# A two-layer transformer step on one core: eight chunks of the adaptive weights come first, sixteen move into the first merge

## The chip, the core and the metric

The kernel runs on one core of a Trainium2 chip. Its time is the device time of one execution, in microseconds (us). TensorE multiplies; ScalarE (ACT), VectorE (DVE) and GpSimd (POOL) work on tiles in SBUF; SyncE (SP) issues the transfers. Each engine runs its own instructions in order and waits for the others on semaphores. [...]

## The reference

The program computes two blocks of two layers each. The change touches the first block only. There, each layer takes a shift, a scale and a gate from a condition vector, for the 256 tokens `x` and the 256 context tokens `ctx`:

```python
for l in range(DEPTH):
    mod = jax.nn.silu(c) @ w_ada[l] + b_ada[l]
    mod_c = jax.nn.silu(c_ctx) @ w_ada[l] + b_ada[l]
    shift, scale, gate = jnp.split(mod[:, None, :], 3, axis=-1)
    ...
    h = rms_norm(x, norm_g[l]) * (1.0 + scale) + shift
    ...
    x_new = x + gate * y
```

`w_ada[l]` is 1024 x 3072. `c` and `c_ctx` are inputs, so the shifts, scales and gates of both layers depend on nothing that the kernel computes before. The gate is wanted only where the layer's output is added to `x`.

## The kernel before

All weights come from one array, `wstream`, in chunks of 1 MB, in the order in which they are used. Four ring buffers hold chunks (`ring`). Each chunk is split for accuracy: ACT rounds it into an upper part `w_hi` (L207, two halves), DVE subtracts to get the rest `w_lo` (L219, two halves), both into the one of two buffers that the chunk's parity picks. TensorE then multiplies three times per weight tile (upper by upper, upper by lower, lower by upper; L261 to L263). SP loads chunk c + 4 once chunk c is split.

A layer of the first block runs in stages, each a block of instructions for every engine that ends when all engines have arrived:

- `ada_stage`: 12 chunks of `w_ada`. The condition vectors (`c_both`, both as upper and lower parts, padded to 128 columns) are the stationary operand and 256 columns of weights stream past (L314, L315); the result is a row of numbers on 4 partitions, copied to `rows` (L476). From the ninth chunk on ACT also squares the eight tiles of `x` (L482), and TensorE sums the squares (L430). In layer 0 the stage also loads `x`, the context, the small parameters and the constants.
- `mod_stage`: TensorE turns the rows into columns (L369, 24 small transposes), ACT takes the inverse root of the mean square (L497, L499), DVE makes `mod` and `scales`, and then multiplies the eight tiles of `x` by the root (L401). In layer 0 a table of biases is also built and stored to device memory (L363), and the stage ends only when the store has landed.
- `glu_stage`: tile by tile, ACT applies scale and shift (L518), POOL rounds the result to `x_hi` (L525), DVE takes the rest `x_lo` (L530), and TensorE starts on tile k of the first chunk when `x_lo` of k is there (`model_norm`).
- the projections and the attention, and then `merge_stage`: 28 chunks (gate, merge and projection for three branches, and four output chunks), each 48 matmuls. Results alternate between the two sides of PSUM. In layer 0 it covers 512 tokens.

For layer 1 the same stages run again, its `ada_stage` directly behind layer 0's `merge_stage`.

## Time and profile before

| | us |
|---|---|
| three runs | 2562.76, 2568.67, 2569.83 |
| median | 2568.67 |
| the profiled execution | 2568.35 |
| its span in the trace | 2566.6 |
| `ada_stage` of layer 0 | 10.0 to 62.6 |
| `mod_stage` of layer 0 | 62.6 to 70.7 |
| `merge_stage` of layer 0 | 352.5 to 676.7 |
| `ada_stage` of layer 1 | 677.3 to 716.4 |
| `mod_stage` of layer 1 | 716.4 to 724.6 |

Stage borders are read from the first instruction of a stage in the trace, in us from the start of the span. A stage's time is what separates its borders; what an engine does inside it costs something only if it is what the stage's end waits for.

### The profile page before, as it was taken

The numbers are of one execution on the slowest core, as the hardware profiler recorded it, in microseconds if no ns is written. First come the engines' busy times: TensorE is split into PE (matmuls) and PEld (weight loads), VectorE is DVE, ScalarE is ACT, GpSimd is POOL, SyncE is SP. The second block draws the span as 40 slices with busy tenths as digits, with TensorE's granted clock in tenths as the row PEclk, the third lists the DMA queues.
The fourth block names the chain that finished last, engine by engine and source line by source line (L and its number), as shares of the span: only waits on it lengthen the run. The fifth ranks groups of instructions, "written<-read, shape, count | busy, mean of one in ns | idle before, by whom it ended". The sixth has DMA issues, their size and how long they took to land. (4 is left out here: it accounts for less than half of the span.)

```text
span 2566.6 us, 45931 instructions
## 1 busy us (share of the span) xinstructions
PE 2408.7 (94%) x17574; PEld 2171.2 (85%) x17574; DVE 1482.7 (58%) x2652; ACT 1247.7 (49%) x1964; POOL 214.3 (8%) x228
## 2 busy tenths in 40 slices
PE   5899899999989999999989999999999988998998
PEld 4678567887767789989987789899899887898998
DVE  4468963333566865655465556554555566565554
ACT  6355654232457565434365454543543564555433
POOL 0013000000002100023000000121121000000220
PEclk9999899999989999999999999999999999999999
DMA  8221022222452125555543234355455442343552
GB/s 334 80 96 70 1 83 93 96 103 88 166 177 96 37 99 181 181 183 193 182 159 116 95 136 164 141 188 183 145 184 193 144 165 83 121 160 132 188 189 98
DMA packets 58453, 354.04 MB, mean 138 GB/s; under 512 B 5904, under 2 KB 16704, under 8 KB 16832
## 3 DMA queue, kind: packets, MB, share of 16 engines
q1 hardware_dynamic: 58160, 351.96, 38.4%
q8 instruction: 104, 1.70, 0.3%
q14 instruction: 45, 0.37, 0.0%
q10 hardware_dynamic: 144, 0.01, 0.0%
HBM read 349.29 MB, written 1.08 MB: 137 GB/s over the span
## 5 line engine op out<-in xcount | busy, mean ns | idle before, releaser
L219 DVE TENSOR_TENSOR w_lo<-ring,w_hi 128x1024 fp32r<-128x1024 f32 x644 | 823.5, 1313 | 517.6 <-ACT w_hi L207 517.4
L261 PE MATMUL psum<-x_hi,w_hi 128*128 128x256 f32 (+1 forms) x3392 | 1043.2, 308 | 60.2 <-DVE x_lo L615 21.9
L263 PE MATMUL psum<-x_hi,w_lo 128*128 128x256 f32 (+1 forms) x3392 | 1024.5, 302 | 0.0
L262 PE MATMUL psum<-x_lo,w_hi 128*128 128x256 f32 (+1 forms) x3392 | 1023.4, 302 | 0.0
L207 ACT ACTIVATE w_hi<-ring 128x1024 fp32r<-128x1024 f32 (+1 forms) x644 | 650.0, 1051 | 299.8 <-PE psum L1573 143.9
L261 PEld LDWEIGHTS psum<-x_hi,w_hi 128*128 128x128 f32 x3392 | 647.4, 191 | 105.5 <-issue 64.7
L262 PEld LDWEIGHTS psum<-x_lo,w_hi 128*128 128x128 f32 x3392 | 648.8, 191 | 27.6 <-issue 2.2
L263 PEld LDWEIGHTS psum<-x_hi,w_lo 128*128 128x128 f32 x3392 | 648.3, 191 | 23.9
L1573 PE MATMUL psum<-h_hi,w_lo 128*128 (+1 forms) x640 | 179.0, 280 | 0.0
L1572 PE MATMUL psum<-h_lo,w_hi 128*128 (+1 forms) x640 | 178.7, 279 | 0.0
L1570 PE MATMUL psum<-h_hi,w_hi 128*128 (+1 forms) x640 | 178.6, 279 | 0.0
L1594 ACT ACTIVATE gate<-psum 128x256 f32<-128x256 f32 x88 | 33.8, 385 | 279.3 <-PE psum L263 279.2
L796 ACT ACTIVATE probT<-psum 128x512 f32<-128x512 f32 (+3 forms) x128 | 79.8, 623 | 179.9 <-PE psum L713 179.2
L1640 POOL CAST h_hi<-hid 128x256 f32 (+1 forms) x88 | 35.0, 397 | 1320.2 <-DVE hid L1613 1320.2
L811 ACT ACTIVATE prob<-prob,neg 128x256 f32<-128x256 f32 (+6 forms) x256 | 127.9, 503 | 34.9 <-DVE neg L764 28.3
L1231 DVE SCALAR_TENSOR_TENSOR conv_out<-cpad,vec,conv_out 128x512 f32<-128x512 f32 (+1 forms) x240 | 142.9, 652 | 0.0
L1613 DVE SCALAR_TENSOR_TENSOR hid<-psum,gate 128x256 f32<-128x256 f32 x88 | 37.4, 425 | 145.6 <-ACT gate L1594 145.5
L1572 PEld LDWEIGHTS psum<-h_lo,w_hi 128*128 128x128 f32 x640 | 120.3, 188 | 0.0
L1573 PEld LDWEIGHTS psum<-h_hi,w_lo 128*128 128x128 f32 x640 | 120.0, 188 | 0.0
L1570 PEld LDWEIGHTS psum<-h_hi,w_hi 128*128 128x128 f32 x640 | 119.8, 187 | 0.0
L1642 POOL TENSOR_TENSOR h_lo<-hid,h_hi 128x256 f32 (+1 forms) x88 | 109.7, 1247 | 13.5 <-POOL h_hi L1640 12.7
L713 PEld LDWEIGHTS psum<-cst,prob 128*128 128x128 f32 (+1 forms) x544 | 60.9, 141 | 44.2 <-DVE prob L771 40.8
(292 smaller groups left out, 2968.6 us busy)
## 6 DMA issues: line engine op xcount, KB each, us to landing
ring<-wstream SPq DMA_DIRECT2D x323, 1024.0 KB, 4.8
x<-xT SPq DMA_DIRECT2D x2, 1024.0 KB, 7.1
x<-ctxT SPq DMA_DIRECT2D x2, 1024.0 KB, 9.9
rel_bias<-bias_by_distance SPq DMA_DIRECT2D x2, 1024.0 KB, 7.6
cst<-consts SPq DMA_DIRECT2D x1, 1662.0 KB, 11.6
kk_sw<-kk_sw SPq DMA_DIRECT2D x8, 128.0 KB, 5.9
out<-x SPq DMA_DIRECT2D x8, 128.0 KB, 2.0
x<-rpb SPq DMA_DIRECT2D x2, 438.0 KB, 5.9
```

The source lines that it names most:

```text
L207: act.activation(w_hi[:, c % 2, h], ring[:, (c + 2 * i) % RING, h], ACT.Copy).then_inc(hi_done.sem, 1)
L219: dve.tensor_tensor(w_lo[:, c % 2, h], ring[:, (c + 2 * i) % RING, h], w_hi[:, c % 2, h].bitcast(F32), ALU.subtract).then_inc(split_done.s ...
L261: pe.matmul(o, w_hi[:, c, w_cols], hi, start=first, stop=False)
L262: pe.matmul(o, w_hi[:, c, w_cols], lo, start=False, stop=False)
L263: return pe.matmul(o, w_lo[:, c, w_cols], hi, start=False, stop=last)
L796: act.activation(self.probT[0:w, v % self.TURNS, :, 0:n], psum[0:w, at:at + wide].rearrange("p (h k) -> p h k", h=2)[:, :, 0:n], ACT.Copy) ...
L811: o = act.activation(p, p, ACT.Exp, bias=self.neg[:, t % 3, half:half + 1], accum_out=self.den[:, t % 3, half:half + 1])
L1231: dve.scalar_tensor_tensor(out=o, in0=src, scalar=wc, in1=o, op0=ALU.mult, op1=ALU.add).then_inc(conv_step.sem, 1)
L1570: pe.matmul(o, w_hi[:, c, b:b + P], h_hi[:, kt, :], start=start and k == 0, stop=False)
L1572: pe.matmul(o, w_hi[:, c, b:b + P], h_lo[:, kt, :], start=False, stop=False)
L1573: mm = pe.matmul(o, w_lo[:, c, b:b + P], h_hi[:, kt, :], start=False, stop=False)
L1642: pool.tensor_tensor(h_lo[:, j, :], hid[:, s, :], h_hi[:, j, :].bitcast(F32), ALU.subtract).then_inc(lower.sem, 1)
```

## The change

Layer 0's `ada_stage` runs 8 chunks (shift and scale) instead of 12. The other 16 (layer 0's gate, 4 chunks, and all 12 of layer 1) are placed in layer 0's `merge_stage`, one behind each main chunk from the third to the eighteenth. Their results go to a free corner of PSUM and then to the first four partitions of `x`, which is not in use there; `x` is loaded again later in the stage. The rows are turned behind main chunks 6 (8 transposes) and 18 (24). Layer 1 has no `ada_stage` and no `mod_stage`: ACT squares `x` during the output chunks, DVE adds the first six of the eight squares into one (five adds), TensorE sums that one and the last two in three matmuls, and the root is taken at the end of `merge_stage`. `c_both` has 4 columns instead of 128 and stays. The multiplication by the root moves, for both layers, from `mod_stage` into `model_norm`, in `glu_stage`, between the `x_lo` steps. The constants come in two parts, and `x` is loaded earlier. In the woven stretch the main chunks all lie in one of the two weight buffers, the ada chunks in the other, so a main chunk's halves are split apart: the first once TensorE has read the first half of the main chunk before (`half_read`), the second once it is done.

```diff
+ADA_FIRST = 8
+ADA_LATER = 2 * ADA_CHUNKS - ADA_FIRST
...
+                    if half_read and n == CB // 2 - 1:
+                        mm.then_inc(half_read.sem, 1)
...
+        def condition(dve, c_both):
+            c0 = conditioned.n
+            upper_half, lower_half = c_both[:, :, 0:2], c_both[:, :, 2:4]
+            dve.tensor_copy(upper_half, c_in[:]).then_inc(conditioned.sem, 1)
+            dve.wait_ge(conditioned.sem, c0 + 1)
+            dve.tensor_tensor(lower_half, c_in[:], upper_half.bitcast(F32), ALU.subtract).then_inc(conditioned.sem, 1)
...
+        def turn_rows(pe, rows, n, at):
+            for t in range(n):
+                mm = pe.transpose(psum[:, at + 4 * t:at + 4 * t + 4], rows[:, t * P:t * P + P], const("ident")[0:4, 0:4])
+            mm.then_inc(rows_turned.sem, 1)
...
-                    dve.wait_ge(rooted.sem, r0 + 2)
-                    for k in range(KT):
-                        dve.tensor_tensor(scratch(k), x[:, k, :], rs[:], ALU.mult).then_inc(scaled_x.sem, 1)
...
+            squares = {5: range(2), 6: range(2, 5), 7: range(5, 8)}
...
+                            sp.dma_start(cst[:, 0:early], consts[:, 0:early]).then_inc(loaded.sem, 16)
                             sp.dma_start(vec[:], vecs).then_inc(loaded.sem, 16)
-                        if j == 6:
-                            sp.dma_start(cst[:], consts[:, 0:N_RESIDENT]).then_inc(loaded.sem, 16)
-                        if j == 7:
-                            rel_sb, bucket, _tab = tables
                             sp.dma_start(rel_sb[:], rel).then_inc(loaded.sem, 16)
                             sp.dma_start(bucket[:], consts[0:32, N_RESIDENT:N_CONST]).then_inc(loaded.sem, 16)
+                        if j == 4:
+                            sp.dma_start(cst[:, early:], consts[:, early:N_RESIDENT]).then_inc(late_consts.sem, 16)
...
+                        pe_stacked(pe, j // 2, j % 2, acc(j % 2, 256)[0:4], lambda k: c_both[:, k, :], True, True)
...
-                for k in range(KT):
-                    dve.wait_ge(upper.sem, u0 + k + 1)
-                    dve.tensor_tensor(x_lo[:, k, :], scratch(k), x_hi[:, k, :].bitcast(F32), ALU.subtract
-                                      ).then_inc(lower.sem, 1)
+                for n in range(KT + 3):
+                    if n < KT:
+                        dve.tensor_tensor(scratch(n), x[:, n, :], rs[:], ALU.mult).then_inc(scaled_x.sem, 1)
+                    k = n - 3
+                    if k >= 0:
+                        dve.wait_ge(upper.sem, u0 + k + 1)
+                        dve.tensor_tensor(x_lo[:, k, :], scratch(k), x_hi[:, k, :].bitcast(F32), ALU.subtract
+                                          ).then_inc(lower.sem, 1)
...
+            later = layer == 0
+            if later:
+                first, gates = 2, ADA_CHUNKS - ADA_FIRST
+                seq, own = [], []
+                for k, chunk_ in enumerate(main):
+                    own.append(len(seq))
+                    seq.append(chunk_)
+                    if first <= k < first + ADA_LATER:
+                        seq.append(("ada", 0, k - first))
+                xf = x[:].rearrange("p k t -> p (k t)")
+                rows = xf[0:4, 0:3 * D]
+                turns = {first + gates: (gates, 0), first + ADA_LATER: (ADA_LATER - gates, 1)}
...
+            def next_two(j, whole, half):
+                if is_ada(j):
+                    half(j + 1, 1)
+                else:
+                    whole(j)
+                if is_ada(j + 1):
+                    half(j + 2, 0)
...
+            def rounds(act, j):
+                def half(k, h):
+                    c = g0[0] + k
+                    if h:
+                        act.wait_ge(chunk_done.sem, c - 1)
+                    else:
+                        act.wait_ge(landed[c % 2].sem, 16 * (c // 2 + 1))
+                        act.wait_ge(half_read.sem, h0 + seq[k - 1][2] + 1)
+                    round_half(act, c, 0, h)
+                next_two(j, lambda k: round_next(act, k // 2, k % 2), half)
...
+                        if j == own[first + ADA_LATER + 2]:
+                            sp.wait_ge(modulated.sem, o0 + 4)
+                            sp.dma_start(x[:, :, 0:S], xT).then_inc(stored.sem, 16)
+                            sp.dma_start(x[:, :, S:2 * S], ctxT).then_inc(stored.sem, 16)
...
+                        if kind == "ada":
+                            pe.wait_ge(acc_free.sem, g0[0] + j - 1)
+                            pe_stacked(pe, j // 2, j % 2, psum[0:4, ada_at(j):ada_at(j) + 256],
+                                       lambda k: c_both[:, k, :], True, True)
+                            continue
...
+                        if later and k in turns:
+                            chunks, which = turns[k]
+                            pe.wait_ge(acc_free.sem, g0[0] + j)
+                            turn_rows(pe, rows, 2 * chunks, side(k) + 1024)
...
+                    if later:
+                        pe.wait_ge(total_squares.sem, ts0 + 5)
+                        for k in (0, 6, 7):
+                            if k:
+                                pe.wait_ge(squared.sem, q0 + 4 + k + 1)
+                            mm = pe.matmul(model_squares, const("ones_model"), y[:, k, :], start=k == 0, stop=k == 7)
+                        mm.then_inc(step.sem, 1)
...
+                    if later:
+                        act.wait_ge(acc_free.sem, g0[0] + n)
+                        model_square(OUT_CHUNKS - 1)
+                        act.wait_ge(step.sem, b0 + 3)
+                        inverse_root(act, model_squares, rs[:], eps_col, r0 + 2)
...
+                    if layer == 0:
+                        sp.wait_ge(scaled_x.sem, scaled_x.n)
...
+            for k, chunk in enumerate(main):
+                put(chunk)
+                if 2 <= k < 2 + ADA_LATER:
+                    ada(*later[k - 2])
```

The order in which instructions stand shows this. First, ACT in layer 0's `merge_stage`, main chunks 5 to 8, counted from 0 (L930 is the sigmoid of a merge chunk, L948 a SiLU on the convolution's output, L926 the SiLU of a gate chunk); before:

```order
L930 ACTIVATE sg<-psum 128x1024
L207 ACTIVATE w_hi<-ring 128x1024 x2
L930 ACTIVATE sg<-psum 128x1024
L948 ACT_TABLE_LOAD
L948 ACTIVATE conv_out<-conv_out,vec 128x512 x4
L207 ACTIVATE w_hi<-ring 128x1024 x4
L926 ACTIVATE prod<-psum 128x1024
L207 ACTIVATE w_hi<-ring 128x1024 x2
```

After, main chunks 5 to 7 (L215 is the rounding, L1021 the copy of an ada chunk's result, L1051 the sigmoid, L1069 the SiLU):

```order
L1051 ACTIVATE sg<-psum 128x1024
L215 ACTIVATE w_hi<-ring 128x1024
L1021 ACTIVATE x<-psum 4x256
L215 ACTIVATE w_hi<-ring 128x1024 x3
L1051 ACTIVATE sg<-psum 128x1024
L1069 ACT_TABLE_LOAD
L1069 ACTIVATE conv_out<-conv_out,vec 128x512 x4
L215 ACTIVATE w_hi<-ring 128x1024
L1021 ACTIVATE x<-psum 4x256
L215 ACTIVATE w_hi<-ring 128x1024 x4
L1021 ACTIVATE x<-psum 4x256
```

Ahead of a main chunk's own step ACT now rounds three halves (both of the ada chunk and the first of the next main chunk); behind it come the other half and the copy.

Second, DVE around layer 0's `mod_stage` and the start of `glu_stage`; before:

```order
L386 TENSOR_TENSOR mod<-psum,vec 128x48
L391 TENSOR_SCALAR vec<-vec 128x2x8 x2
L391 TENSOR_SCALAR vec<-vec 128x2x24
L394 TENSOR_TENSOR mod<-psum,mod 128x48
L396 SCALAR_TENSOR_TENSOR scales<-mod,vec 128x16
L401 TENSOR_TENSOR nk<-x,rs 128x512 x4
L401 TENSOR_TENSOR nv<-x,rs 128x512 x4
L358 UNCONDITIONAL_BRANCH
L1174 UNCONDITIONAL_BRANCH
L530 TENSOR_TENSOR x_lo<-nk,x_hi 128x512 x4
L530 TENSOR_TENSOR x_lo<-nv,x_hi 128x512 x4
```

After (L540 is the multiplication by the root, L544 the `x_lo` step; the branches are the border between the stages):

```order
L395 SCALAR_TENSOR_TENSOR scales<-mod,vec 128x16
L402 UNCONDITIONAL_BRANCH
L1329 UNCONDITIONAL_BRANCH
L540 TENSOR_TENSOR nk<-x,rs 128x512 x4
L544 TENSOR_TENSOR x_lo<-nk,x_hi 128x512
L540 TENSOR_TENSOR nv<-x,rs 128x512
L544 TENSOR_TENSOR x_lo<-nk,x_hi 128x512
L540 TENSOR_TENSOR nv<-x,rs 128x512
L544 TENSOR_TENSOR x_lo<-nk,x_hi 128x512
L540 TENSOR_TENSOR nv<-x,rs 128x512
L544 TENSOR_TENSOR x_lo<-nk,x_hi 128x512
L540 TENSOR_TENSOR nv<-x,rs 128x512
```

The eight multiplications have crossed the border, and four of them stand between `x_lo` steps. SP's loads of the bias rows (`rpb`) in layer 0 wait for all eight.

Third, ACT from the last output chunk of layer 0 to layer 1's `glu_stage`, after (L1010 squares two tiles of `x` into `y`, L507 and L509 are the root, L528 is scale and shift); before, twelve chunks of rounding and copying stood between the last L207 and the L497:

```order
L215 ACTIVATE w_hi<-ring 128x1024 x2
L1010 ACTIVATE y<-x 128x512 x4
L507 ACTIVATE rs<-psum,consts_small 128x512
L509 ACT_TABLE_LOAD
L509 ACTIVATE rs<-rs 128x512
L937 UNCONDITIONAL_BRANCH
L1304 UNCONDITIONAL_BRANCH
L528 ACTIVATE nk<-nk,mod,scales 128x256 x8
```

## Rows read from the trace of the kernel before

**Rows 1.** The page, part 1: busy time of TensorE.

```profile
PE 2408.7 (94%) x17574; PEld 2171.2 (85%) x17574; DVE 1482.7 (58%) x2652; ACT 1247.7 (49%) x1964; POOL 214.3 (8%) x228
```

**Rows 2.** Stretches by stage; the first line names the columns.

```profile
core 0: us, PE busy (x) PEld busy (x) DVE busy (x) ACT busy (x) POOL busy (x), PEclk, DMA share, GB/s
10.00:62.60 52.60, 37.00 (x208) 29.55 (x208) 29.42 (x27) 32.84 (x45) 0.00 (x0) 0.90 0.90 350
62.60:70.70 8.10, 2.57 (x27) 1.66 (x26) 5.65 (x14) 3.18 (x4) 0.00 (x0) 0.76 0.02 6
70.70:86.40 15.70, 12.99 (x49) 10.54 (x50) 9.39 (x10) 9.93 (x19) 6.16 (x10) 0.80 0.64 174
352.50:674.90 322.40, 318.99 (x1360) 257.40 (x1360) 116.54 (x111) 100.03 (x102) 0.00 (x0) 0.99 0.27 98
674.90:677.30 2.40, 0.10 (x1) 0.00 (x0) 1.69 (x5) 0.00 (x0) 0.00 (x0) 1.00 0.00 0
677.30:716.40 39.10, 35.27 (x208) 29.20 (x208) 29.31 (x27) 32.53 (x45) 0.00 (x0) 0.91 0.82 315
716.40:724.60 8.20, 1.63 (x25) 1.55 (x24) 5.50 (x11) 2.61 (x4) 0.03 (x1) 0.64 0.09 38
724.60:735.60 11.00, 8.37 (x49) 8.24 (x50) 8.20 (x10) 9.86 (x18) 6.11 (x10) 0.65 0.65 177
```

**Rows 3.** Stretches of the start, for the transfer rate.

```profile
0.00:35.00 35.00, 19.54 (x128) 17.68 (x128) 20.07 (x21) 22.02 (x27) 0.20 (x4) 1.00 0.90 338
15.00:20.00 5.00, 4.46 (x32) 3.99 (x32) 4.56 (x5) 4.47 (x7) 0.00 (x0) 1.00 0.69 249
35.00:45.00 10.00, 5.11 (x32) 4.53 (x32) 5.40 (x5) 7.33 (x10) 0.00 (x0) 0.89 1.01 425
```

**Rows 4.** Timeline of ACT, layer 0: start, length, instruction, idle before.

```profile
35.10 2.00 ACT L207 ACTIVATE w_hi<-ring 128x1024 fp32r<-128x1024 f32 x2 [3.19 <-DMA ring<-wstream]
...
59.48 1.13 ACT L482 ACTIVATE nv<-x 128x512 f32<-128x512 f32 x2
62.91 0.69 ACT L497 ACTIVATE rs<-psum,consts_small 128x512 f32<-128x512 f32 x1 [2.29 <-PEq L433]
...
65.53 0.59 ACT L380 ACTIVATE tab_sb<-psum 16x511 f32<-16x511 f32 x1
```

**Rows 5.** Timeline of TensorE, layer 0: the first sum of squares, and the transposes.

```profile
50.25 1.22 PE L430 MATMUL psum<-nk,cst 128*128 128x512 f32 x1 [5.94 <-DMA bucket<-consts]
...
62.92 1.61 PE L369 MATMUL psum<-cst,rows 4*128 4x4 f32 x24 [0.32 <-PEq L433]
```

**Rows 6.** DMA issues, 60 to 80 us: size, median us to landing.

```profile
x<-rpb SPq DMA_DIRECT2D x2, 438.0 KB, 5.9
bias_by_distance<-tab_sb SPq DMA_DIRECT2D x1, 31.9 KB, 1.6
```

**Rows 7.** Timeline of TensorE, layer 1's last ada chunk and the sums behind it.

```profile
711.74 0.28 PE L315 MATMUL psum<-w_lo,c_both 128*128 128x256 f32 x1
...
712.71 0.28 PE L315 MATMUL psum<-w_lo,c_both 128*128 128x256 f32 x1
712.82 3.60 PE L430 MATMUL psum<-nv,cst 128*128 128x512 f32 x8
```

**Rows 8.** Timeline of DVE, layer 0's last output chunk to layer 1's first.

```profile
675.04 1.66 DVE L1099 SCALAR_TENSOR_TENSOR x<-psum,mod,x 128x256 f32<-128x256 f32 x4 [7.06 <-PE psum L263]
...
719.38 2.50 DVE L401 TENSOR_TENSOR nk<-x,rs 128x512 f32<-128x512 f32 x4 [0.33 <-ACT rs L499]
...
726.39 0.69 DVE L530 TENSOR_TENSOR x_lo<-nk,x_hi 128x512 fp32r<-128x512 f32 x1 [2.10 <-POOL x_hi L525]
...
730.79 3.73 DVE L530 TENSOR_TENSOR x_lo<-nv,x_hi 128x512 fp32r<-128x512 f32 x4
```

**Rows 9.** Timeline of ACT in layer 0's merge: a SiLU, and two gate chunks.

```profile
439.31 2.94 ACT L948 ACTIVATE conv_out<-conv_out,vec 128x512 f32<-128x512 f32 x4
...
459.15 1.03 ACT L926 ACTIVATE prod<-psum 128x1024 f32<-128x1024 f32 x1 [8.92 <-PE psum L263]
...
470.13 1.03 ACT L926 ACTIVATE prod<-psum 128x1024 f32<-128x1024 f32 x1 [8.06 <-PE psum L263]
```

**Rows 10.** Timeline of DVE in the same merge: behind a projection chunk.

```profile
503.35 2.36 DVE L990 TENSOR_TENSOR prod<-psum,sg 128x1024 f32<-128x1024 f32 x2 [6.88 <-issue]
505.63 2.35 DVE L1000 TENSOR_TENSOR y<-y,prod 128x1024 f32<-128x1024 f32 x2
```

More of the change, by code:

```diff
@@ L360, in _ @@
                 def _(sp):
[L361 to L364 removed]
+                    sp.wait_ge(read.sem, read.n + 2)
+                    sp.dma_start(table, tables[2][:]).then_inc(loaded.sem, 16)
+                    sp.wait_ge(loaded.sem, lb + 16)
                 @block.tensor
                 def _(pe):
[L368 to L373 removed]
+                    turn_rows(pe, rows, 2 * KT, 0)
+                    pe.matmul(psum[0:2 * HEADS, 2048:2048 + 511], tables[0][:], tables[1][:], start=True, stop=True
+                              ).then_inc(read.sem, 1)
                 @block.scalar
@@ L433, in ada_stage @@
+            rows_turned.n += 1
+            modulated.n += 2
+            rooted.n += 2
+            read.n += 2
+            loaded.n += 16
+        def ada_stage(rows, scratch, tables):
+            n = ADA_FIRST
+            c0, q0, x_loaded = conditioned.n, squared.n, stored.n + 32
+            squares = {5: range(2), 6: range(2, 5), 7: range(5, 8)}
+            early = CONSTS["ones_conv"][0]
             with nc.Block() as block:
@@ L467, in _, with sum_squares @@
-                    mm.then_inc(step.sem, 1)
+                    def sum_squares(k):
+                        if k == 0:
+                            pe.wait_ge(loaded.sem, loaded.n + 64)
+                        pe.wait_ge(squared.sem, q0 + k + 1)
+                        pe.matmul(psum[:, 1024:1024 + 2 * S], const("ones_model"), scratch(k), start=k == 0,
+                                  stop=k == KT - 1)
+                    pe.wait_ge(conditioned.sem, c0 + 2)
+                    for j in range(n):
+                        pe_acc(pe, j // 2, j % 2)
+                        pe_stacked(pe, j // 2, j % 2, acc(j % 2, 256)[0:4], lambda k: c_both[:, k, :], True, True)
+                        for k in squares.get(j - 1, ()):
+                            sum_squares(k)
@@ L469, in _ @@
+                    for k in squares[n - 1]:
+                        sum_squares(k)
                 @block.scalar
@@ L1021, in merge_stage @@
             rooted.n += 2
+            if later:
+                half_read.n += ADA_LATER
+                rows_turned.n += 2
+                modulated.n += 4
+                total_squares.n += 5
+                step.n += 1
+                rooted.n += 2
+                squared.n += KT
             for c in (centred, squared, scaled_x, affine):
@@ L1034, in build @@
         c_in = sb("c_in", [P, KT, 2])
-        mod = sb("mod", [P, 3 * KT, 2])
+        c_both = sb("c_both", [P, KT, 4], F32R)
+        mods = [sb("mod", [P, 3 * KT, 2]) for _ in range(DEPTH)]
+        sb("half_line", [P, HALF_LINE])
         scales = sb("scales", [P, KT, 2])
@@ L1122, in _ @@
                 def _(sp):
+                    if layer == 0:
+                        sp.wait_ge(scaled_x.sem, scaled_x.n)
                     for a in range(2):
@@ L2425, in merge, with ada @@
             put(_cols(w_proj, _r(512 * h, 512)))
+    def ada(l, c):
+        put(_rows(v["w_ada"][l], _r(256 * c, 256)))
     for l in range(DEPTH):
         w = v["w_in"][l]
-        for c in range(0, 3 * D, 256):
-            put(_rows(v["w_ada"][l], _r(c, 256)))
+        if l == 0:
+            for c in range(ADA_FIRST):
+                ada(0, c)
+            later = [(0, c) for c in range(ADA_FIRST, ADA_CHUNKS)] + [(1, c) for c in range(ADA_CHUNKS)]
         span(w, A_VAL, 1024)
```

275 lines of the change are left out of this document (151 added, 124 removed).

## The prediction

> **What bounds the kernel now.** I read the page first: TensorE is busy for 94% of the span [rows 1], so what can be won lies where it is not, or where it does work of little use. The stretches by stage show where that is [rows 2]. Layer 0's merge is full: 319.0 us busy of 322.4, and two gate chunks end 10.98 us apart [rows 9], for 48 matmuls each. The two ada stages are different. Layer 0's takes 52.6 us with TensorE busy 37.0, at a transfer rate of 350 GB/s; layer 1's takes 39.1 us, and neither ACT (32.5) nor DVE (29.3) nor the transfers fill it: its chunks go by the chain rounding, rest, matmuls, copy. In both mod stages (8.1 and 8.2 us) TensorE has 2.6 and 1.6 us of work.
>
> Layer 0's start is bound by transfers. The timeline of ACT shows a wait of 3.2 us for a ring chunk before the rounding at 35.10 [rows 4], and TensorE waits 5.9 us, until 50.25, for the last constants before its first sum of squares [rows 5].
>
> **Layer 0's start.** The chunk that gates the new stage is the ninth (the first of `glu_stage`), since ACT rounds it ahead of the copy of the eighth. Ahead of it now stand nine chunks, `x` and the context, 0.13 MiB of constants, 0.71 of parameters and 0.06 of the table: 11.9 MiB, 12.5 MB. Before, 338 GB/s over 35 us moved 11.8 MB [rows 3]; the stretch of 249 GB/s from 15 to 20 us, where no free ring buffer and no other load stood in the queue, is now filled by `x` and the context, worth 0.7 MB. So the ninth chunk lands at about 35, as before. Then, in order: two halves of rounding 2.0 [rows 4], the copy 0.3, three squares 1.7 (two take 1.13, rows 4), the last sum 0.9 (eight rows of matmul, four sums, take 3.60 [rows 7]): 39.9. With 0.3 to the next stage, the root and the table's copy take 3.2 (62.91 to 66.1, rows 4), and the store 0.3 to issue and 1.6 to land [rows 6], which is 45.3. The 16 transposes, 1.1 (24 take 1.61, rows 5), lie beside the root.
>
> That store follows the twelfth chunk in SP's queue. By then 16.4 MiB, 17.2 MB, have been asked for; by the rates of rows 3 16.1 MB were moved by 45, and with the 0.7 of the refilled gap the queue is empty at 46. The store alone took 1.6 us, in an empty queue [rows 2, 6]. [...] No run here shows the store in a full queue. I take 47 for the start of `glu_stage`, against 70.7: **-23.7 us**. [...]
>
> The removed memset and the stage border ahead of the first chunk (about 1.6 us) are hidden under the transfers.
>
> **The root inside `glu_stage`.** Before, the eight multiplications took 2.50 for four, 0.62 each, with POOL idle [rows 8]. Now the first x tile reaches ACT 0.65 later, and DVE has two steps per tile. What a step costs beside POOL's rounding is seen in `x_lo`: four in 3.73, of which the last, after POOL's end, takes 0.68, so 1.02 each beside a rounding against 0.62 alone [rows 8]. The rounding thus costs DVE 0.4 per tile. Per tile 0.62 + 0.62 + 0.4 = 1.64, where ACT's pace was 1.0. Four multiplications first (2.9 with one rounding), five tiles at 1.64, three more `x_lo` at 0.65 and a wait of about 0.3: the last `x_lo` at 13.3 us after the stage's start. In layer 1 it was about 9.9 (724.6 to 730.79 + 3.73). TensorE's first chunk has 256 tokens there, goes at ACT's pace, and ends 0.8 behind the last tile: **+3.2 us**, bounds +1.0 (no cost of POOL's, only the first tile's delay and part of a step) and +5.5. In layer 0, with 512 tokens, TensorE is the slower one: at 0.229 us per matmul (10.98 / 48) six take 1.37 per tile, more at the low clock, and it ends 15.7 after the start of the stage [rows 2]; now 16.4. The bias rows are loaded once the eighth multiplication is done, about 9.5 in, and land 1.3 + 5.9 later [rows 6], at 16.7, where the matmuls that follow the first chunk want them: another 0.4. Queued behind that wait on SP are loads of ring chunks, three of which are already in; nobody waits for them. **+1.3 us**, bounds +0.6 and +3.5.
>
> The row shows a DVE instruction with two inputs in SBUF stretched by POOL's. [...]
>
> **Sixteen ada chunks in the merge.** The 16 matmuls of 256 columns follow each other at 0.12 us (eight steps from 711.74 to 712.71, rows 7): 1.94 per chunk. I take 1.95, **+31.2 us**; the bounds are 1.7 (if the load of 4 columns instead of 128 is what sets the step) and 2.5 (layer 1's stage spent about 32 us on its twelve, 2.6 each, where ACT and DVE set the pace). The 32 transposes add 32 x 0.067 = **+2.1** [rows 5].
>
> Is the next main chunk split in time? TensorE needs its first half 1.95 us after the end T of the main chunk before, and the second half 5.5 later, at T + 7.4. The first half is rounded from the middle of the previous chunk on, five us early. The second is rounded after T. Behind a projection DVE has 2.36 + 2.35 [rows 10] and then 1.2: T + 5.9. The worst place is main chunk 6: sigmoid 1.0, a table load of 1.3 and a SiLU of 2.94 [rows 9] stand ahead of the rounding of 1.0 and the rest of 1.2, T + 7.5, and the eight transposes give 0.5 back. So no wait, with 1.5 us to spare at the projections and almost none at chunk 6. ACT gets 2.4 and DVE 2.4 more per main chunk of 13 us, of which they have 100 and 117 of 322 busy [rows 2]. Transfers in the stretch go from 98 GB/s to about 160, under the 425 of rows 3.
>
> **Layer 1's start.** The last output chunk's matmuls end at 674.9 [rows 2]. Then DVE's update 1.66 [rows 8] with 0.15 of waking, two squares 1.13, the last sum 0.9, 0.3 to wake ACT, the root 2.6 (62.91 to 65.53, rows 4) and the border with its waits 0.7: 7.5 us. The other squares, adds and sums lie beside the output chunks. So `glu_stage` starts at 674.9 + 31.2 + 2.1 + 7.5 = 715.7 on the old scale, against 724.6: **-8.9 us**.
>
> **The sum**, against the profiled execution's 2568.35 (0.3 under the median): -23.7 + 1.3 - 8.9 + 3.2 = -28.1, which gives **2540 us**. The gain is mostly layer 0's: there the four chunks, and the waits for constants, leave the stretch that transfers bind. In layer 1 the stages' 47.3 us are bought with 33.3 of full TensorE time, 5.1 more of tail than the 2.4 before, and 3.2 in the next stage. So most of the work is only moved.
>
> **Rivals.**
> A. A woven chunk costs what it did in its own stage, 2.6 instead of 1.95, because TensorE waits at each switch between operands or for late halves. For it: chunk 6 has no slack, and at every switch there are new semaphore waits. Against it: between main chunks no time is lost, 48 steps fill the 10.98. It gives 16 x 0.65 = +10.4: 2551.
> B. The start is later: the late constants and chunks ten to twelve are in the same engines as the ninth chunk and the store, and the clock is low there. For it: before, the constants took long to land and held TensorE to 50.25. `glu_stage` starts at 51 or 52: 2545.
> C. The other side: the clock. In the woven stretch the array works a seventh of the time with 4 of its columns; if the clock fell at each woven chunk, as it does where TensorE idles (PEclk 0.64 and 0.76 in the mod stages, rows 2), the main chunk behind it would go like layer 0's first, which at 0.80 in its stretch was busy for 13.0 instead of 11.0, and the woven one at half speed, 1.9 more. That is 3.9 x 16 = 62: 2602. From 1.75 us per woven chunk on, the kernel is slower than before. Against it: in layer 1's ada stage the mean was 0.91, with TensorE busy for 35 of 39 us, and the main chunks keep it busy for 11 us of every 13.
> D. That the change doesn't do what it says: the order shows the stages gone and the root's multiplications past the border, so this has no chance.
>
> **How the numbers follow.** The forecast 0.62, with its own range 2532 to 2547; A 0.16; B 0.12; C 0.04; the rest, 0.06, for a heavier stall at the half-wise splitting, up to losing the gain. Range 2531 to 2554. Differences under 0.3% (7.7 us) can't be told from no change here, so faster means under 2561: the forecast, A, B and a third of the rest, 0.91; same 0.05, slower 0.04.
>
> **What would show it.** Each step has its place in the profile after. Layer 0's first scale and shift on ACT at 47 (before: behind 70.7), its first `glu_stage` chunk ending 16.8 after; the tile period of DVE near 1.6, not 1.0; the distance between ACT's ends of two main chunks in the woven stretch 12.9 instead of 11.0, with no wait of TensorE for `w_lo` over 0.1; 7.5 us between the last output matmul and the first scale and shift of layer 1. The prediction is wrong if the woven distance is over 13.5, if PEclk falls in the merge, or if `glu_stage` of layer 0 starts after 51.

## The result, and the profile after

| | before | changed |
|---|---|---|
| median of 4 runs, us | 2568.57 | 2537.56 |
| lowest to highest, us | 2562.76 to 2569.83 | 2531.99 to 2546.52 |
| profiled execution (span), us | 2568.35 (2566.6) | 2546.52 (2544.7) |
| ratio, with its 95% interval | | 0.989, 0.987 to 0.991 |

The changed kernel is faster, by 31 us in the medians where 28 were forecast; a second set of runs, told below, gave 25. Its profiled execution is the slowest of its four. The stages that the change touches can be read from it all the same; what its last 1640 us add is told below.

The stages of the kernel after, to be laid beside [rows 2]; the columns are the same. PEclk is TensorE's granted clock as a share of its full one; in all 13 traces it is 1.00 or 0.50 at any moment, and what lies between are means:

```profile
9.80:42.90 33.10, 25.29 (x144) 13.49 (x144) 19.15 (x18) 23.62 (x33) 0.00 (x0) 1.00 1.02 400
42.90:48.30 5.40, 2.19 (x18) 1.17 (x18) 0.71 (x6) 3.08 (x4) 0.00 (x0) 0.70 0.57 206
48.30:66.70 18.40, 14.14 (x49) 11.44 (x50) 14.94 (x18) 10.33 (x19) 6.99 (x10) 0.72 0.39 108
330.90:684.50 353.60, 350.37 (x1649) 280.03 (x1650) 158.84 (x153) 141.06 (x157) 0.00 (x0) 0.99 0.37 137
684.50:691.80 7.30, 2.99 (x7) 0.85 (x5) 1.66 (x4) 3.75 (x5) 0.00 (x0) 1.00 0.00 0
691.80:706.40 14.60, 9.85 (x49) 8.79 (x50) 13.87 (x18) 10.32 (x18) 7.04 (x10) 0.65 0.50 134
```

From these and [rows 2] the whole difference up to the end of layer 1's first chunk can be added up:

| step | forecast | this profile |
|---|---|---|
| start of layer 0's `glu_stage`, 70.7 to 48.3 | -23.7 | -22.4 |
| its first chunk, 15.7 to 18.4 | +1.3 | +2.7 |
| from there to the merge, untouched | 0 | -1.9 |
| the merge, 322.4 to 353.6 | +33.3 | +31.2 |
| last output chunk to layer 1's `glu_stage`, 49.7 to 7.3 | -42.2 | -42.4 |
| its first chunk, 11.0 to 14.6 | +3.2 | +3.6 |
| sum | -28.1 | -29.2 |

**Layer 0's start.** ACT's long waits are for ring chunks, and the ninth chunk is rounded at 36.23 (the forecast had 35); after that the stage is closed by the squares, by TensorE's sums (the last end at 42.03) and by SyncE. ACT's timeline, answering to [rows 4]:

```profile
27.27 2.00 ACT L215 ACTIVATE w_hi<-ring 128x1024 fp32r<-128x1024 f32 x2 [3.18 <-DMA ring<-wstream]
32.29 2.00 ACT L215 ACTIVATE w_hi<-ring 128x1024 fp32r<-128x1024 f32 x2 [1.71 <-DMA ring<-wstream]
36.23 2.00 ACT L215 ACTIVATE w_hi<-ring 128x1024 fp32r<-128x1024 f32 x2
38.41 1.65 ACT L491 ACTIVATE nv<-x 128x512 f32<-128x512 f32 x3
43.18 0.69 ACT L507 ACTIVATE rs<-psum,consts_small 128x512 f32<-128x512 f32 x1 [3.12 <-PEq L443]
45.72 0.57 ACT L419 ACTIVATE tab_sb<-psum 16x511 f32<-16x511 f32 x1
```

SyncE's, of the same stretch; the first row ends at 42.76 with the issue of the twelfth chunk, and that is where the ada stage ends; the second is the table's store:

```profile
32.33 10.43 SPq L201 DMA_DIRECT2D ring<-wstream  x3
46.31 0.34 SPq L406 DMA_DIRECT2D bias_by_distance<-tab_sb  x1
```

**The gated stage.** DVE now alternates two instructions, and they repeat every 1.62 us (54.99 to 56.60 to 58.23; this is a second profile of the changed kernel, in which the stage begins 0.05 later). The `x_lo` step (L544) takes 1.09; the multiplication (L540) takes 0.68, which is what either takes alone. Alone they follow each other at 0.62 [rows 8]:

```profile
54.39 0.68 DVE L540 TENSOR_TENSOR nv<-x,rs 128x512 f32<-128x512 f32 x1
54.99 1.09 DVE L544 TENSOR_TENSOR x_lo<-nk,x_hi 128x512 fp32r<-128x512 f32 x1
56.00 0.68 DVE L540 TENSOR_TENSOR nv<-x,rs 128x512 f32<-128x512 f32 x1
56.60 1.09 DVE L544 TENSOR_TENSOR x_lo<-nk,x_hi 128x512 fp32r<-128x512 f32 x1
58.23 3.31 DVE L544 TENSOR_TENSOR x_lo<-nv,x_hi 128x512 fp32r<-128x512 f32 x4
```

**The merge.** Two ends of gate chunks are now 12.83 apart on ACT, where they were 10.98 [rows 9]. Between them stand the late half of the rounding, the woven chunk's copy, and then the next rounding with 3.27 of idle time to spare:

```profile
448.64 1.03 ACT L1047 ACTIVATE prod<-psum 128x1024 f32<-128x1024 f32 x1 [4.38 <-PE psum L271]
449.56 1.05 ACT L215 ACTIVATE w_hi<-ring 128x1024 fp32r<-128x1024 f32 x1
450.51 0.36 ACT L1021 ACTIVATE x<-psum 4x256 f32<-4x256 f32 x1
450.77 1.99 ACT L215 ACTIVATE w_hi<-ring 128x1024 fp32r<-128x1024 f32 x2
456.03 1.06 ACT L215 ACTIVATE w_hi<-ring 128x1024 fp32r<-128x1024 f32 x1 [3.27 <-PE psum L271]
461.47 1.03 ACT L1047 ACTIVATE prod<-psum 128x1024 f32<-128x1024 f32 x1 [4.37 <-PE psum L271]
```

**Layer 1's start** is the short chain of update, squares, sums and root, of all engines:

```profile
684.69 1.66 DVE L1251 SCALAR_TENSOR_TENSOR x<-psum,mod,x 128x256 f32<-128x256 f32 x4 [5.88 <-PE psum L271]
686.38 1.15 ACT L1010 ACTIVATE y<-x 128x512 f32<-128x512 f32 x2 [9.79 <-DVE x L1251]
687.07 1.98 PE L1003 MATMUL psum<-y,cst 128*128 128x512 f32 x4 [1.56 <-ACT y L1010]
689.09 0.69 ACT L507 ACTIVATE rs<-psum,consts_small 128x512 f32<-128x512 f32 x1 [1.55 <-PE psum L1003]
```

**Behind it** no edit stands, yet of the 29.2 us this profile keeps only 21.9 at its end. Most of the 7.3 is lost in one place: TensorE is busy without a break and runs at half clock, where the kernel before did the same work at the full one. Two copies of ACT that mark this place are 12.97 apart here and 7.82 before, so 5.1 us go there. The kernel before, and the changed one:

```profile
1335.00:1340.00 5.00, 5.00 (x47) 5.00 (x46) 3.58 (x7) 1.22 (x3) 0.00 (x0) 1.00 0.74 223
```

```profile
1306.00:1311.00 5.00, 5.00 (x25) 5.00 (x25) 3.59 (x7) 0.86 (x1) 0.00 (x0) 0.50 0.82 238
1311.00:1316.00 5.00, 5.00 (x25) 5.00 (x25) 0.00 (x0) 0.41 (x2) 0.00 (x0) 0.50 0.44 182
```

Ahead of the fall, over 1299.0 to 1304.6, TensorE had 3.6 us of work in 5.6. The kernel before had a gap of the same kind (2.7 us of work in the five from 1330 to 1335) and kept its full clock. Why one falls and the other doesn't stays open.

I added up the half-clock stretches behind layer 1's first merge chunk in all 13 profiles of this study, and set them against the time from there to the end. They are 52 to 91 us, and the time 1634.4 to 1645.5, with a correlation of 0.74: the more half clock, the longer. The kernel before has the least of it (52.5 us, 1634.4), but with its loads reordered it has 62.6 and 1636.8, and one variant of the changed kernel 67.8 and 1635.5. So there is a spread of some 10 us between single profiles in stages that no edit touches, and the clock goes with about half of its variation; the rest isn't explained. The medians of the runs do better, and below I compare stages rather than spans wherever an effect is under 5 us.

### The profile page after: what moved, and what is told of

The parts are those of the page before. It is cut to its first block and busy times, and to the rows that moved or that the text cites. A ratio compares the mean times of both kernels' runs of the same rounds, so it can differ in the third digit from the quotient of the medians.

```text
span 2544.7 us, 45688 instructions
## 1 busy us (share of the span) xinstructions
PE 2403.7 (94%) x17564; PEld 2157.0 (85%) x17564; DVE 1485.0 (58%) x2655; ACT 1248.2 (49%) x1964; POOL 214.9 (8%) x228
## 5 line engine op out<-in xcount | busy, mean ns | idle before, releaser
L269 PE MATMUL psum<-x_hi,w_hi 128*128 128x256 f32 (+1 forms) x3392 | 1046.3, 308 | 57.4 <-DVE x_lo L629 21.9
L215 ACT ACTIVATE w_hi<-ring 128x1024 fp32r<-128x1024 f32 (+1 forms) x644 | 651.7, 1051 | 322.0 <-PE psum L271 152.4
```

Of the source, the lines that this page charges most:

```text
L215: act.activation(w_hi[:, c % 2, h], ring[:, (c + 2 * i) % RING, h], ACT.Copy).then_inc(hi_done.sem, 1)
L269: pe.matmul(o, w_hi[:, c, w_cols], hi, start=first, stop=False)
```

## The experiments

Where a stage is compared, the marks are the starts of ACT's instructions: the root's first (the logarithm, Ln), the first scale and shift, and the copy that follows the first chunk.

**Root in PSUM.** The forecast had put 0.4 us per tile on POOL's cast; this takes the root, one of the multiplication's two inputs, out of SBUF.

```diff
-            act.activation(rs, rs, ACT.Exp, scale=-0.5)
+            act.activation(rs if out is None else out, rs, ACT.Exp, scale=-0.5)
...
-                        dve.tensor_tensor(scratch(n), x[:, n, :], rs[:], ALU.mult)
+                        dve.tensor_tensor(scratch(n), x[:, n, :], psum[:, root_at:root_at + 2 * S], ALU.mult)
```

> The same work as the changed kernel; only the root that the eight multiplications read lies in PSUM instead of SBUF (ACT's Exp writes it there, in both layers). Theory: a DVE instruction with both inputs in SBUF and POOL's cast hold each other up, and nothing else makes the tile period 1.62 us, where its two DVE instructions alone take 0.62 each. With one input in PSUM the multiplication runs beside the cast, and only x_lo meets it: period about 1.25 to 1.3, first chunk of layer 1's glu_stage 12.3 to 12.8 us after the stage's start instead of 14.6, so about 2 us less; layer 0's first chunk is set by TensorE's matmuls (18.4 us in the changed kernel, much of it at the low clock) and moves by under 1. Rival: the period comes from the chain DVE - ACT - POOL - DVE, three tiles deep; then it stays at 1.62 and nothing moves. Second rival: reading PSUM costs DVE more than it saves, and the period grows.

DVE's timeline, to be laid beside the rows of the gated stage above:

```profile
52.55 0.69 DVE L544 TENSOR_TENSOR x_lo<-nk,x_hi 128x512 fp32r<-128x512 f32 x1
53.16 0.68 DVE L540 TENSOR_TENSOR nv<-x,psum 128x512 f32<-128x512 f32 x1
53.76 0.69 DVE L544 TENSOR_TENSOR x_lo<-nk,x_hi 128x512 fp32r<-128x512 f32 x1
54.36 0.68 DVE L540 TENSOR_TENSOR nv<-x,psum 128x512 f32<-128x512 f32 x1
54.96 1.06 DVE L544 TENSOR_TENSOR x_lo<-nk,x_hi 128x512 fp32r<-128x512 f32 x1
```

The period is 1.21, and 1.59 where one `x_lo` still meets a cast. Layer 1 goes from Ln to the end of its first chunk in 15.1 us instead of 17.4 (17.35 in the second profile), layer 0 in 21.2 instead of 23.5 and 23.1. The chain as cause falls, and so does a dear PSUM. Layer 0 gains 2 us, where under 1 was expected, but not all of that is the edit's: TensorE is at half clock for 6.8 us around this chunk, and for 13.7 and 10.2 in the two profiles of the changed kernel. What is left at an equal clock is told under both edits. Over the whole, 2537.95 against the 2537.56 of the changed kernel (ratio to before 0.9885, 0.9848 to 0.9923): 4 us are within its spread.

**The store not awaited**, and the twelfth load issued a stage later.

```diff
+                    load_one(sp, 0, -1)
                     sp.wait_ge(read.sem, read.n + 2)
-                    sp.dma_start(table, tables[2][:]).then_inc(loaded.sem, 16)
-                    sp.wait_ge(loaded.sem, lb + 16)
+                    sp.dma_start(table, tables[2][:]).then_inc(table_stored.sem, 16)
...
-                        load_one(sp, j // 2, j % 2)
+                        if j < n - 1:
+                            load_one(sp, j // 2, j % 2)
```

> The same work; in layer 0's mod stage SyncE no longer waits for the table's store to land (waited for later, ahead of the next writers of its buffer), and the load of the twelfth chunk, on whose issue (42.76 us) the ada stage ends, is issued at the head of the mod stage instead. Theory: glu_stage of layer 0 starts when SyncE is through, 48.3 in the changed kernel; the wait for the store is worth 1.7 and the late issue 0.7 to 0.8, so it starts at 45.8 to 46.1 and everything behind it comes 2.4 earlier. Rival: the stage also waits for ACT's root and copy (46.3), so only the store's part less 0.3 is gained; and a second: the first chunk of glu_stage runs more of its time at the low clock, starting earlier, and gives part of it back.

From Ln to the first scale and shift it takes 4.6 us instead of 5.9: 1.25 gained, the first rival's size (1.7 less what SyncE and ACT still take). The first scale and shift is at 49.1 as in the changed kernel, not the 2.4 earlier that was expected, since here the ninth chunk was rounded 2 us later (38.21 against 36.23): the ring's landings differ by that much between runs. The late issue proved worth 0 to 0.6: ACT idles 2.48 ahead of Ln here and 3.12 there, but 2.50 also in the variant with the root in PSUM, which issues it early. The runs show no gain: 2543.29 (4 runs; ratio to before 0.9888, 0.9855 to 0.9920), where the changed kernel has 2537.56 and 2540.55. The store now stands right behind a ring chunk in the queue, and landed 3.6 us after its issue; in the changed kernel the chunk was nearly through and it took 1.6:

```profile
ring<-wstream SPq DMA_DIRECT2D x1, 1024.0 KB, 6.5
bias_by_distance<-tab_sb SPq DMA_DIRECT2D x1, 31.9 KB, 3.6
```

So the store took 2.0 us more where the chunk ahead of it had 3.4 still to go. In the changed kernel it took no more: the twelfth chunk was issued at 42.42 and landed 4.9 later, 1.0 behind the store's issue, and the store landed in 1.6 all the same, as in the empty queue of [rows 6]. Over 46 to 47 the rate had fallen to 188 GB/s, and over 47 to 48 to 33.

**Twelve chunks first.** The gate's four stay at the start.

```diff
-ADA_FIRST = 8
+ADA_FIRST = 12
...
-                turns = {first + gates: (gates, 0), first + ADA_LATER: (ADA_LATER - gates, 1)}
+                turns = {first + ADA_LATER: (ADA_LATER, 0)}
```

> The gate's four chunks of layer 0 stand again at the start (12 chunks there, 12 woven instead of 16). Theory: at the start a chunk costs its transfer, 1 MiB at 400 GB/s = 2.6 us, in the merge its 16 matmuls, 1.83. So glu_stage of layer 0 starts 10.5 us later (58.8, and 0.5 for eight more transposes), the merge is 7.3 + 0.5 shorter: the kernel is about 3 us slower than the changed one. Rival: the start gains far more from early loads and little from the four chunks, and the start moves by under 8 us, so that the place of these chunks is worth nothing. Rival two: each woven chunk costs more than its matmuls (late halves), the merge shrinks by over 9 us and the kernel is not slower.

The first scale and shift comes at 66.1 instead of 49.1, so 17 us later, not 11, and the merge (from its first SiLU to layer 1's first scale and shift, with one half-clock stretch of 3.4 as in the second profile of the changed kernel) is 6.8 shorter. By the stages that loses 10 us, three times the 3 expected. The kernel takes 2550.59 (5 runs; ratio to before 0.9948, 0.9926 to 0.9969), 10 and 13 above the two medians of the changed kernel. So a chunk at the start costs 4.1 to 4.3 us, not its 2.6 of transfer. The rows show what else stands there, but no run parts it: ACT waits for TensorE too, TensorE runs at half clock in parts, and in the code a ring chunk is only asked for once the chunk two before it has landed:

```profile
36.43 2.00 ACT L215 ACTIVATE w_hi<-ring 128x1024 fp32r<-128x1024 f32 x2 [0.96 <-DMA ring<-wstream]
42.40 2.00 ACT L215 ACTIVATE w_hi<-ring 128x1024 fp32r<-128x1024 f32 x2 [3.71 <-DMA ring<-wstream]
48.24 0.37 ACT L486 ACTIVATE rows<-psum 4x256 f32<-4x256 f32 x1 [1.38 <-PE psum L327]
```

Over 40 to 45 the transfers moved 308 GB/s (422 in the five before), and over 45 to 50 the mean granted clock was 0.72.

**Before, with the loads reordered.**

```diff
+                        if j == 0:
+                            sp.dma_start(x[:, :, 0:S], xT).then_inc(stored.sem, 16)
+                        if j == 1:
+                            sp.dma_start(x[:, :, S:2 * S], ctxT).then_inc(stored.sem, 16)
...
+                            sp.dma_start(cst[:, early:], consts[:, early:N_RESIDENT]).then_inc(late_consts.sem, 16)
...
+                            sp.dma_start(cst[:, 0:early], consts[:, 0:early]).then_inc(loaded.sem, 16)
...
-                        if j == 6:
-                            sp.dma_start(cst[:], consts[:, 0:N_RESIDENT]).then_inc(loaded.sem, 16)
```

> The kernel before with only its loads in layer 0's ada stage reordered as in the changed one: x and the context behind the first and second ring chunk, the first part of the constants, the parameters and the table's inputs behind the third, the late constants behind the fifth with a semaphore of their own. Theory: TensorE's wait to 50.25 us goes, but the twelve chunks still take their time: with twelve chunks at the start the changed kernel read the root at 59.6, against 62.9 in the kernel before, so about 3 us are gained and no more; the four chunks less were worth 16 of the 22. Rival: the wait for the constants was what held the stage, and 6 us or more are gained by the order of the loads alone. It is also a second look at the stages that no edit touches, in the manner of the kernel before.

The root is read at 61.4 instead of 62.9, and the kernel takes 2564.85 (10 runs) against 2569.17: ratio 0.9977, 0.9951 to 1.0003, which is not told from no change. TensorE's wait to 50.25 is gone and 1.5 us come of it, half of the 3 expected and less than the 2 us by which the ring's landings differ between runs. That wait ran beside the ring's own pace.

**Root apart.** Eight multiplications in a stage of their own, ahead of `glu_stage`.

```diff
+                    dve.wait_ge(rooted.sem, r0)
+                    for k in range(KT):
+                        dve.tensor_tensor(scratch(k), x[:, k, :], rs[:], ALU.mult).then_inc(scaled_x.sem, 1)
```

> The root's eight multiplications stand in a stage of their own ahead of glu_stage, in both layers, as they stood before the change; all else as changed. Theory: they cost 8 x 0.62 = 5.0 us and a stage border of 0.3 to 1 ahead, and give back what they cost inside: layer 1's first chunk ends 11.0 after the stage's start instead of 14.6 (-3.6), layer 0's up to 2.7 earlier, depending on the clock. So 1.4 to 2.4 us slower per layer, 3 to 5 in the whole. Rival: the two DVE steps held up by POOL's cast cost as much as the stage of their own (5 against 5), and nothing changes: then applying the root in the gated stage was worth nothing. The period of x_lo alone should fall to ACT's pace of 1.0 per tile.

From Ln to the first chunk's end: layer 0 26.1 instead of 23.5 and 23.1, layer 1 19.2 instead of 17.4. So it is 2.6 to 3.0 and 1.8 to 1.9 slower, 4.4 to 4.9 in all, and in the runs 2546.68 against 2540.55 of the changed kernel on the same chip (0.9917, 0.9898 to 0.9936, and 0.9889, 0.9872 to 0.9906). The rival is out: applying the root in the gated stage pays, in spite of POOL.

**A quarter of each woven chunk.** This kernel leaves out 12 of a woven chunk's 16 matmuls, so what it computes is not the program's result; it serves to measure what the weave costs.

```diff
-            for k in range(KT):
+            for k in range(KT) if few is None else few:
...
-                                       lambda k: c_both[:, k, :], True, True)
+                                       lambda k: c_both[:, k, :], True, True, (0, KT // 2))
```

> Of each woven chunk's 16 matmuls only 4 are done (two of its eight slices of rows), so the modulation of layer 0's gate and of layer 1 is computed from a part of its terms. Theory: TensorE is the only engine that a woven chunk costs anything: 16 x 12 matmuls of 0.114 us go, 21.9 us. Then the halves have 1.4 us less time: needed at T + 6.0 where DVE is through behind a projection at T + 5.9 and behind main chunk 6 at T + 7.5, so one wait of about 1.5 us shows up at chunk 6 and 21.9 - 1.5 = 20.4 is gained over the changed kernel. Rival: the weave costs time in the switches and in the splitting by halves beside its matmuls; then the main chunks' distance does not shrink by 1.37 (12.83 to 11.46) but by less, in all of the chunks.

From the first SiLU to layer 1's first scale and shift: 328.5 with one half-clock stretch of 3.4 us in it, which costs about 1.7, an estimate, half of it; so 326.8, against 347.0 in the one profile of the full weave that had none. That is 20.2 shorter, with 20.4 expected, and the kernel takes 2519.89 (4 runs; ratio to before 0.9821, 0.9793 to 0.9849). The one wait for `w_lo` that the merge then has is behind main chunk 6, 0.92 long, where 1.5 was expected:

```profile
416.52 2.94 ACT L1069 ACTIVATE conv_out<-conv_out,vec 128x512 f32<-128x512 f32 x4
419.37 1.04 ACT L215 ACTIVATE w_hi<-ring 128x1024 fp32r<-128x1024 f32 x1
420.44 4.70 DVE L227 TENSOR_TENSOR w_lo<-ring,w_hi 128x1024 fp32r<-128x1024 f32 x4 [9.37 <-ACT w_hi L215]
421.72 0.51 PE L269 MATMUL psum<-op_hi,w_hi 128*128 128x512 f32 x1 [0.92 <-DVE w_lo L227]
```

So the weave costs its matmuls and, as far as these stages resolve it, nothing beside them, and the place with no slack is the one that the forecast named.

**The changed kernel again**, on the chip of the next two.

> The changed kernel itself, on the same chip as the variants below. Its stages other than the ones in dispute should repeat: layer 0's glu_stage starts at 48.3 to 50 (the landing of the ring chunks was up to 2.5 us apart in four variants with the same start), its period of two DVE steps stays 1.62, the merge 347 to 351 from the first SiLU to layer 1's first scale and shift, median 2534 to 2542. What differs between this profile and the first one of the same kernel is what no edit explains.

2540.55 (5 runs), ratio 0.9889, 0.9872 to 0.9906. The period and layer 1's first chunk repeat to 0.06 us; layer 0's first chunk ends 0.4 sooner behind Ln (23.1 against 23.5). The merge takes 348.6 against 350.6, with 3.4 us at half clock against 6.8, and the rest 1645.3 against 1643.8.

**Both edits.** Root in PSUM, and the store not awaited; nothing else.

> The two edits together: root in PSUM in both layers, and in layer 0 the table's store not awaited, with the twelfth load issued a stage later. From the single ones: 1.25 us earlier start of layer 0's glu_stage, 1 to 2 off its first chunk, 2.2 off layer 1's first chunk: 4 to 5 us under the changed kernel, if the two do not cover each other. Rival: the start of layer 0's first chunk is at the low clock, so the earlier start and the faster tiles there are given back, and 2.2 to 3 us are left.

> The kernel of the two edits once more, on the same chip as the next: median 2531 to 2538.

2533.35 (4 runs; ratio to before 0.9875, 0.9858 to 0.9892), and again 2536.16 (6 runs; 0.9876, 0.9844 to 0.9909). From Ln to the first chunk's end 21.0 and 15.1, against 23.1 and 17.4: 4.4 us by stages, 7 in the medians of one chip. In layer 0 the two profiles compared have the same half-clock stretch, 10.2 us, so the 2.1 there is the edits': 1.25 of the store and about 0.9 of the root in PSUM, the "under 1" that was expected of it. The marks leave out what stands ahead of Ln; there these two profiles idle 3.4 and 3.5, against 2.5 and 3.1, behind sums of which the first ran at half clock. The intervals overlap those of the changed kernel, so it is the stages that show it.

**TensorE kept busy**, on top of both.

```diff
+                pe.matmul(psum[:, at:at + 256], const("ones_model"), cst[:, 0:256], start=True, stop=True)
```

> The kernel of the two edits, and in four stretches in which TensorE waits (layer 0's mod stage, the end of the merge ahead of the last sums and behind them, the head of glu_stage in both layers) it multiplies a constant tile into a free PSUM bank: 12, 10, 12 and 14 matmuls of 256 columns. Theory: TensorE's granted clock, 0.72 on the mean in the first chunk of layer 0 and 0.65 in layer 1's, falls because TensorE has nothing to do in the mod stages; kept busy it stays at the full one, and layer 0's first chunk, whose 48 matmuls of 512 columns take twice as long at the low one, ends up to 2.5 us earlier; layer 1's, which goes by ACT's pace, by under 0.5. Rival: the clock has fallen for another reason, or the added matmuls hold up what they stand ahead of (the stage's border, the sums), and it is no faster or 1 to 3 us slower.

It was slower, 2544.53 (6 runs; 0.9918, 0.9903 to 0.9933). The clock did stay full there (PEclk 1.00 over 43 to 60 and over 684 to 706), but each of these matmuls runs as two of 0.227 us, and they stood in the way: 12 took 5.45 us in the mod stage and 14 took 6.28 ahead of the first chunk, which ended 25.1 behind Ln instead of 21.0. From the last squares to layer 1's first scale and shift it took 11.4 us instead of 6.3. Hence the next:

> As the kernel that kept TensorE busy, but sized to the gaps: a matmul of the constant tile runs as two of 0.227 us, so 12 and 14 of them took 5.45 and 6.28 us and held up the stages they stood in. Now 4 in the mod stage, 7 at the head of glu_stage, 3 and 5 around the last sums of the merge. Theory: the clock stays at the full one as in that run, TensorE's first matmul of layer 0's first chunk starts with the first x_lo and the 48 take 11.0 to 11.6, so the chunk ends 2 to 2.5 us earlier than in the kernel of two edits (17.1 us after DVE's first multiplication there), layer 1's 0.3 to 0.8 earlier: about 2.5 to 3 us in all. Rival: the clock falls all the same since the gaps are not filled without a break, or it falls elsewhere later instead, and the total does not move.

The clock over layer 0's first chunk, first with both edits, then with TensorE also kept busy:

```profile
48.00:53.00 5.00, 0.31 (x1) 0.34 (x2) 3.63 (x6) 3.47 (x8) 1.76 (x4) 0.50 0.34 139
53.00:58.00 5.00, 5.00 (x13) 3.83 (x13) 5.00 (x9) 4.90 (x11) 4.00 (x6) 0.51 0.00 2
```

```profile
48.00:53.00 5.00, 4.68 (x20) 3.81 (x21) 4.74 (x8) 4.06 (x9) 2.71 (x5) 1.00 0.05 20
53.00:58.00 5.00, 5.00 (x23) 4.05 (x23) 5.00 (x8) 4.90 (x9) 4.07 (x6) 1.00 0.10 17
```

Thirteen matmuls in five microseconds against 23. From Ln to the end of layer 0's first chunk it is 19.0 instead of 21.0, the expected 2; layer 1's first chunk does not move (15.1): it goes at DVE's pace, and TensorE waits in it four times for an `x_lo`, 1.2 us in all. The half-clock stretch at this place, 6.8 to 13.7 us long and begun between 45.0 and 66.8 in all eleven profiles without such matmuls, is missing in both with them.

What follows can't be put down to the added matmuls. Between the first chunk and the merge of layer 0 it takes 277.2 instead of 273.3: the half-clock stretch from 232 on is 13.7 us long instead of 6.8, and one more appears near 106. But the changed kernel's first profile and the one with the root in PSUM have the long stretch too, and the latter takes 277.1. In layer 1 the chunks behind the first, up to the first of the merge, take 192.8 instead of 197.0, but with twelve chunks first, and no such matmuls, they take 192.8 as well. So whether the rival was partly right, that the clock falls elsewhere later instead, stays open. The runs: 2531.25 (6 runs; 0.9866, 0.9835 to 0.9896), 5 under both edits alone on the same chip and 6 to 9 under the changed kernel, the lowest of all that do the whole work. That it beats the two edits alone rests on medians whose intervals overlap, and on the 2 us of one chunk.

## Why the prediction was right

The sign, the size and the two large terms were right: the start (-22.4 for -23.7) and layer 1's two stages against the weave (-42.4 and +31.2 for -42.2 and +33.3). Step by step:

- **The start, 47 forecast, 48.3 found.** The sum gave 45.3, and the 47 that I took from it held 1.7 more, my estimate, for a store that lands behind the twelfth chunk and for what might come late. No run shows that 1.7: the store landed in 1.6, so the wait did not come, and with the store not awaited it took 3.6 behind a chunk that had 3.4 to go. In its place the ninth chunk was rounded 1.2 later; behind it the last sums ended at 42.03, 1.1 more, since I had let one sum follow the last square, but the eight sums in one row take 3.6 us; and SyncE was still issuing until 42.76, 0.7 more. That these 3.0 came out near the 1.7 is luck. The root, the table and the store took what I had.
- **Where that gain comes from was only half right.** I spoke of four chunks "and the waits for constants". The runs part it: the four chunks 17 us (twelve first), the loads 1.5 (before, reordered), the root's place 4.4 (root apart, where the first scale and shift came at 53.5 instead of 49.1). They sum to 22.9 for the 22 us; each is from one profile, and the 1.5 is within what the landings differ by. The forecast reached the total of the step by the ninth chunk's landing, which doesn't ask what a chunk costs; priced at their 2.6 of transfer the four chunks would have been over 6 us short, as my expectation for twelve chunks first was.
- **The root in the gated stage.** The period of 1.64 was found as 1.62, and layer 1's +3.2 as +3.6. So the row's 0.4 per rounding held. With the root in PSUM the period was 1.21: that the root lay in SBUF is what made the 0.4. In layer 0 I had +1.3 and it was +2.7: TensorE was at half clock for about 4 us longer than before (mean 0.72 of 18.4 us against 0.80 of 15.7), which the step had named ("more at the low clock") but priced at nothing. With TensorE kept busy, and so at the full clock, the chunk took 2 us less.
- **The woven chunks.** 1.95 was forecast from [rows 7], 1.83 found, so 29.3 for 31.2. That is the mis-sized term: a step is 0.114 to 0.115 instead of 0.119 to 0.121. The operand that is loaded has 4 columns instead of 128, and its load takes 84 to 90 ns instead of 204. The same shows in layer 0's ada stage (0.115 against 0.120). That the one comes of the other is likely, but no run changes the columns alone. I had left this at the lower bound, whose 1.7 per chunk was my estimate and stands in no row. The transposes (+2.1) were right.
- **Slack** at chunk 6 was called almost none. In the changed kernel nothing waits there; with 1.4 us less it waits 0.9.
- **The rivals.** A (2.6 per woven chunk) is out by the distance of 12.83. B (start at 51 to 52) did not come: `glu_stage` starts at 48.3 and 48.4 in the two profiles of the changed kernel, though the landings of the ring moved the start of some variants by up to 2 us. C (the clock falls in the weave) is out: mean 0.99 over the merge, and 1.00 in one variant (the store not awaited, 331 to 688). D is out.
- What the forecast did not have is the spread of the half-clock stretches in untouched stages. It moves a single execution by more than any of the errors above, and it is most of why this profile shows 22 us and the medians 31. The stages sum to 29.2, and the two sets of medians gave 31 and 25, so that the first came within 3 us of the forecast is partly luck; the agreement by stages is not.

## What to carry to other kernels

Work that is small for the full engine but waits on everything in a stage of its own was cheaper here between large pieces of the same engine: sixteen chunks that took 2.6 to 4.2 us each in stages of their own cost 1.83 woven, as long as every late half has its slack counted at the busiest place. Price a removed step by the pace of the stage that it stood in, not by its bytes: a chunk at the start cost 4.1 to 4.3 us here, and its transfer 2.6. When a DVE instruction is moved beside a POOL one, look whether one of its inputs can lie in PSUM: here it took the pair from 1.62 to 1.21 us. And where an effect is smaller than what the clock's stretches move, some 10 us between single profiles here, compare marks within a stage, not spans.

## What the runs showed of the hardware

- Two DVE instructions in turn, beside POOL's casts: 1.62 us per pair with both inputs of both in SBUF, 1.21 with one input of one of them in PSUM. A DVE instruction with both inputs in SBUF that started while a cast ran took 1.06 to 1.09 instead of 0.68, and the multiplication with the root in PSUM 0.68 there too. A cast that started while one with both in SBUF ran took 0.84 to 1.05 instead of 0.61.
- A 32 KB store issued 3.1 us behind a 1 MiB load in the same queue, while that was still to land: 3.6 us (the store not awaited). It took 1.6 where the load had 1.0 left (the changed kernel).
- A matmul of the constant tile, 256 columns wide and fp32, appears as two of 0.227 us (TensorE kept busy: 12 in 5.45 us).
- TensorE's clock went to half (PEclk 0.50) at both starts of the changed kernel: at 45.0 in layer 0's mod stage, where TensorE had 2.2 us of work in 5.4, and at 693.6 in layer 1, behind 7.3 us with 3.0 of work. With constant matmuls in the gaps it stayed full through both (1.00 over 43 to 58 and 684 to 706 with the short ones). Once fallen it stayed at half for up to 13.7 us, even with TensorE busy for 13 of them (1304.6 to 1318.2).
